# Output projection of prompt tiles 0 to 4 moved into the mixer steps of a two-layer hybrid decoder kernel

## What is computed

```python
def trunk_layer(x, ...):
    xn = rmsnorm(x, norm_mix)
    (...) = split_cols(xn @ w_in)                  # 1024 -> 2644 columns
    y_a, ... = rglru_mixer(...)                    # 256 wide, recurrent
    y_b = attn_fn(q, k, v, qi, ki, wi)             # 512 wide, top-256 sparse attention
    y_c, ... = gla_mixer(...)                      # 256 wide, linear attention
    x = x + jnp.concatenate([y_a, y_b, y_c], axis=-1) @ w_out   # 1024 x 1024
    hid = rmsnorm(x, norm_mlp) @ w_up              # 1024 -> 4096
    x = x + jnp.square(jax.nn.relu(hid)) @ w_down
    return x, ...
```

## Time and profile before

| | us |
|---|---|
| runs | 4073.2, 4067.2, 4069.69 (median 4069.69) |
| the profiled execution, first to last instruction | 4072.7 (no other time of it is shown) |
| mixer steps 3 to 7 of layer 0, by the starts of their L1109 | 92.3, 94.5, 101.5, 107.0, 116.3 long |
| output stage of layer 0, first L1382 to first L1389 | 134.0 |

### The profile page before, as it was taken

How to read it: one execution, slowest core, us unless ns; L and a number is a source line. 1 busy time by engine, 2 the same in 40 slices (tenths; PEclk the granted TensorE clock), 3 DMA queues, 4 the chain that set the end, 5 groups by cost and what they waited for, 6 DMA issues and landing times.

```text
span 4072.7 us, 52249 instructions
## 1 busy us (share of the span) xinstructions
PE 3569.3 (88%) x17850; PEld 2698.7 (66%) x17850; DVE 2124.8 (52%) x4881; ACT 1018.2 (25%) x2269; POOL 474.9 (12%) x637
## 2 busy tenths in 40 slices
PE   5778778888799999999987787787787999999999
PEld 3545555556447999999855554555464489999997
DVE  1347778877523444434323577887773334343344
ACT  2232333233401111111123233333234011111110
POOL 0100000221301000000001000002122000000000
PEclk9888888775999999999998888876768999999999
DMA  4000000237621111111410000002465201111111
GB/s 137 15 21 14 14 11 9 46 56 140 208 80 52 42 42 42 54 51 42 140 46 22 14 14 14 11 14 60 41 173 183 88 32 57 48 42 42 42 42 55
DMA packets 189759, 229.61 MB, mean 56 GB/s; under 512 B 72723, under 2 KB 150613, under 8 KB 189493
## 3 DMA queue, kind: packets, MB, share of 16 engines
q1 hardware_dynamic: 161796, 165.17, 15.1%
q0 software_dynamic: 20416, 50.27, 3.9%
q10 hardware_dynamic: 7280, 10.83, 0.8%
HBM read 203.22 MB, written 22.98 MB: 56 GB/s over the span
## 4 chain that ended last, share of the span: by engine, by line
PE 74%; DVE 10%; issue 5%; ACT 5%; DVEq 2%; SPq 1%; DMA 1%; POOLq 1%; POOL 1%; ACTq 0%
PE bank L1389 13%; PE bank L1390 13%; PE bank L1391 13%; PE bank L1096 10%; PE bank L1382 6%; PE bank L1092 5%; PE bank L1194 4%; DVE arena L1454 2%; ACT arena L709 2%; PE bank L1178 2%; DVE arena L1721 1%; PE bank L1186 1%; PE bank L1307 1%; PE bank L1140 1%; SPq L464 1%
## 5 line engine op out<-in xcount | busy, mean ns | idle before, releaser
L1861 DVE TENSOR_TENSOR x_rows<-x_rows,bank 128x512 f32<-128x512 f32 (+1 forms) x576 | 396.1, 688 | 632.1 <-PE bank L1391 632.1
L1096 PE MATMUL bank<-arena 128*128 128x512 f32 (+5 forms) x1440 | 526.5, 521 | 3.0 <-ACT arena L737 1.5
L1454 DVE TENSOR_SCALAR_CACHE_REDUCE arena<-arena,vectors 128x384 bf16<-128x384 f32 (+7 forms) x434 | 500.0, 1152 | 47.5 <-POOLq L406 15.3
L709 ACT ACTIVATE arena<-bank 128x512 f32<-128x512 f32 (+11 forms) x848 | 325.1, 440 | 772.3 <-PE bank L1096 334.0
L1389 PE MATMUL bank<-xT_hi,w_up_hi 128*128 128x364 f32 (+1 forms) x1536 | 506.0, 329 | 5.3 <-DVE vectors L1842 5.3
L1391 PE MATMUL bank<-xT_hi,w_up_lo 128*128 128x364 f32 (+1 forms) x1536 | 506.0, 329 | 0.0
L1390 PE MATMUL bank<-xT_lo,w_up_hi 128*128 128x364 f32 (+1 forms) x1536 | 505.9, 329 | 0.0
L1389 PE MATMUL bank<-w_down_hi,hidden_hi 128*128 128x512 f32 x1152 | 449.5, 390 | 7.5 <-issue 7.5
L1390 PE MATMUL bank<-w_down_lo,hidden_hi 128*128 128x512 f32 x1152 | 449.6, 390 | 0.0
L1391 PE MATMUL bank<-w_down_hi,hidden_lo 128*128 128x512 f32 x1152 | 449.6, 390 | 0.0
L1096 PEld LDWEIGHTS bank<-arena 128*128 128x128 f32 (+1 forms) x1440 | 254.5, 194 | 254.8 <-issue 226.4
(11 more groups left out here) (251 smaller groups left out, 4369.4 us busy)
## 6 DMA issues: line engine op xcount, KB each, us to landing
w_up_landing<-in_w_up SPq DMA_DIRECT2D x32, 1024.0 KB, 7.3
w_down_landing<-in_w_down SPq DMA_DIRECT2D x32, 1024.0 KB, 4.9
arena<-in_cache_k SPq DMA_DIRECT2D x160, 128.0 KB, 2.7
arena<-in_cache_v SPq DMA_DIRECT2D x160, 128.0 KB, 2.6
arena<-in_cache_v POOLq DMA_DIRECT2D x96, 128.0 KB, 3.1
arena<-in_cache_k POOLq DMA_DIRECT2D x96, 128.0 KB, 2.9
arena<-in_w_in ACTq DMA_DIRECT2D x4, 2048.0 KB, 16.1
out_projection<-in_w_out SPq DMA_DIRECT2D x16, 512.0 KB, 9.7
```

Of the source, the lines that this page charges most:

```text
L709: return act.activation(dst, src, ACT.Copy, scale=scale)
L1096: ins = mm(b[:R, o:o + w], xnT[:, c, 0:R], w_in[:, c, c0:c0 + w], start=c == 0, stop=c == 7)
L1454: ts(junk, sc, cf[:R].bitcast(F32), None, ALU.is_ge, ALU.add, accum_out=cnt[:R])
L1861: tt(x, x, b[P - R:P, :], ALU.add).then_inc(s_took, 1)
```

## The change

`EARLY = 5`: for tiles a = 0 to 4 the product y @ w_out leaves the output stage and is done in mixer step s = a + 3, as four bursts of 256 columns (8 products each): op0 and op1 in slot 0, op2 in slot 2, op3 in slot 8. A quarter of w_out (1 MB) is loaded by SyncE into the one buffer wq before each burst. ScalarE copies the burst's bank into one of two buffers `part`, and a GpSimd DMA adds it to x in `x_scratch` in DRAM (in layer 0 the prompt's first 640 rows are copied there first). The attention transposes `yb` move from slot 1 to slot 0, the attention parts of tiles 0 to 4 are no longer stored, and the output order changes. The SBUF for it (3072 columns) comes from a smaller scratch area for GpSimd's DMAs.

```diff
-OUT_ORDER = (0, NT) + tuple(range(1, NT))
+EARLY = 5
+OUT_ORDER = (0, NT, 2, 5, 1, 3, 6, 4, 7)
...
+def projects(s):
+    return s - 3 if 0 <= s - 3 < EARLY else None
...
+                if h == 0:
+                    if attends(s - 1) is not None:
+                        act.append((l, attends(s - 1), "yb"))
+                    if projects(s) is not None:
+                        act += [(l, projects(s), "op0"), (l, projects(s), "op1")]
...
+                    sp.dma_start(x_scr[0:EARLY * P, :], D["x_prompt"].rearrange("a t d -> (a t) d")[0:EARLY * P, :]).then_inc(s_xcp, 16)
...
+                def load_quarter(a, q):
+                    if q:
+                        sp.wait_ge(s_full_a, A_AT[l, a, f"op{q - 1}"] + 1)
+                    elif a or l:
+                        sp.wait_ge(s_full_a, A_AT[(l, a - 1, "op3") if a else (l - 1, EARLY - 1, "op3")] + 1)
+                    sp.dma_start(wq, D["w_out"][l].rearrange("(c p) n -> p c n", p=P)[:, :, 256 * q:256 * q + 256]).then_inc(s_wq, 16)
+                    if q == 0:
+                        sp.wait_ge(s_yst, T(l, a) + 1)
+                        for i, c in enumerate((0, 6)):
+                            sp.dma_start(yac[:, 2 * i:2 * i + 2, :], y_scr[a].rearrange("p (c r) -> p c r", c=8)[:, c:c + 2, :]).then_inc(s_yac, 16)
+                load_x(1)
+                for s in range(TILES - 1):
+                    a = projects(s)
+                    if a is not None:
+                        for q in (1, 2):
+                            load_quarter(a, q)
+                    if s + 2 < TILES:
+                        load_x(s + 2)
+                    if a is not None:
+                        load_quarter(a, 3)
+                    if projects(s + 1) is not None:
+                        load_quarter(projects(s + 1), 0)
...
+                    if t == 7:
+                        sp.wait_ge(s_full_d, D_AT[l, 5, "r1"] + 1)
                         sp.dma_start(yTl[:, t % 2, :, :], y_scr[t].rearrange("p (c r) -> p c r", c=8)).then_inc(s_y[t % 2], 16)
                     if t == 1:
                         sp.wait_ge(s_full_d, D_AT[l, NT, "r1"] + 1)
-                    sp.dma_start(xall[:R, t, :], x_src(l, t)).then_inc(s_xr[t], 16)
+                    if t == 0:
+                        for i in range(2):
+                            sp.wait_ge(s_acc[i], 16 * part_n(l + 1, 0, 0) // 2)
+                    sp.dma_start(xall[:R, t, :], x_scr[t * P:(t + 1) * P, :] if t < EARLY else x_src(l, t)).then_inc(s_xr[t], 16)
                     if t == 0:
                         sp.dma_start(gml, D["norm_mlp"][l].partition_broadcast(P)).then_inc(s_gml, 16)
-                    if t == 1:
+                    if t == 5:
                         load_up(0)
...
+                def add_part(a, q):
+                    pool.wait_ge(s_evac, A_AT[l, a, f"op{q}"] + 1)
+                    pool.dma_start(x_scr[a * P:(a + 1) * P, 256 * q:256 * q + 256], part[:, q % 2, :], accum_op=ALU.add).then_inc(s_acc[q % 2], 16)
                 rstd(0)
+                if l == 0:
+                    pool.wait_ge(s_xcp, 16)
...
+                            add_part(projects(s), q)
                     if s == NT:
                         pool.wait_ge(s_pt, 16 * (l + 1))
@@ -627,11 +695,13 @@
                         load_ki(3)
                     if s + 1 < TILES:
                         rstd(s + 1)
-                    if attends(s - 1) is not None:
+                    if attends(s - 1) is not None and attends(s - 1) >= EARLY:
                         a = attends(s - 1)
                         pool.wait_ge(s_evac, A_AT[l, a, "yb"] + 1)
                         store(y_part(a, 2, 4), yB)
                         stored(s_ybst)
+                    if projects(s) is not None:
+                        add_part(projects(s), 2)
...
+                                add_part(projects(s), 3)
                             pool.wait_ge(s_evac, A_AT[l, t, "yc"] + 1)
                             store(y_part(t, 6, 2), yC[:, t % 2, :, :])
...
+                def part_out(a, q):
+                    n = part_n(l, a, q)
+                    if n >= 2:
+                        act.wait_ge(s_acc[q % 2], 16 * (n // 2))
+                    b = take((l, a, f"op{q}"))
+                    copy(part[:, q % 2, :], b[:, 0:256]).then_inc(s_evac, 1)
...
+                        if h == 0 and attends(s - 1) is not None:
+                            a = attends(s - 1)
+                            if l * (NT - EARLY) + max(a - EARLY, 0):
+                                act.wait_ge(s_ybst, l * (NT - EARLY) + max(a - EARLY, 0))
+                            b = take((l, a, "yb"))
+                            copy(yB, b[:, :].rearrange("p (c r) -> p c r", c=4)).then_inc(s_evac, 1)
...
+                        if h == 0 and projects(s) is not None:
+                            for q in range(2):
+                                part_out(projects(s), q)
...
+                                part_out(projects(s), 2)
                             if P_:
                                 decay_logits(s)
...
                                 project(s + 1, 7)
+                            if projects(s) is not None:
+                                part_out(projects(s), 3)
                             if P_:
                                 R = rows(s)
                                 b = take((l, s, "yc"))
...
+                    if t < EARLY:
+                        act.wait_ge(s_xr[t], 16 * (l + 1))
+                    else:
+                        act.wait_ge(s_took, D_AT[l, t, "r1"] + 1)
...
+                def project_out(a, q):
+                    pe.wait_ge(s_wq, 16 * (part_n(l, a, q) + 1))
+                    if q == 0:
+                        pe.wait_ge(s_yac, 32 * (l * EARLY + a + 1))
+                        evac((l, a, "yb"))
+                    b = a_bank((l, a, f"op{q}"))
+                    for c in range(8):
+                        y = yB[:, c - 2, :] if 2 <= c < 6 else yac[:, c if c < 2 else c - 4, :]
+                        ins = mm(b[:, 0:256], y, wq[:, c, :], start=c == 0, stop=c == 7)
+                    ins.then_inc(s_full_a, 1)
...
+                        if h == 0 and attends(s - 1) is not None:
+                            attention_T(attends(s - 1))
                         if h == 1:
-                            if attends(s - 1) is not None:
-                                attention_T(attends(s - 1))
                             if P_:
                                 heads_T(s)
                         if h == 2:
+                            if projects(s) is not None:
+                                project_out(projects(s), 2)
                             if P_:
...
                             probs_T(A_, h - 1)
                         if h < 7 and A_ is not None:
                             logits(A_, h + 1)
+                        if h == 0 and projects(s) is not None:
+                            for q in range(2):
+                                project_out(projects(s), q)
                         if h >= 1 and A_ is not None:
                             values(A_, h - 1)
...
                             if N_:
                                 project(s + 1, 7)
+                            if projects(s) is not None:
+                                project_out(projects(s), 3)
                             if P_:
                                 R = rows(s)
                                 pe.wait_ge(s_yc, T(l, s) + 1)
...
+                    for n in range(2 if t >= EARLY else 0):
                         b = d_bank((l, t, f"r{n}"))
...
-                                pe.wait_ge(s_xT, 2 * (TILES * l + min(TILES, (c0 + w + P - 1) // P + 1)))
+                                pe.wait_ge(s_xT, 2 * (TILES * l + order_covers(range(c0 // P, (c0 + w + P - 1) // P))))
...
-    nc = _bacc.Bacc("TRN2", target_bir_lowering=False, num_devices=1)
+    nc = _bacc.Bacc("TRN2", target_bir_lowering=False, num_devices=1, dynamic_dma_scratch_size=4096)
...
```

More of the change, by code:

```diff
@@ L57, in selects, with order_covers @@
     return s - 1 if 2 <= s - 1 < NT else None
+def projects(s):
+    return s - 3 if 0 <= s - 3 < EARLY else None
+def order_covers(tiles):
+    return max(OUT_ORDER.index(t) for t in tiles) + 1
 def rows(t):
@@ L94, in plan @@
                 if h == 2:
+                    if projects(s) is not None:
+                        act.append((l, projects(s), "op2"))
                     if P_:
@@ L131, in plan @@
                         act.append((l, s + 1, "G3"))
+                    if projects(s) is not None:
+                        act.append((l, projects(s), "op3"))
                     if P_:
@@ L212, in program @@
         ARENA = (53215 - const_cols - 288 - 16) // 8 * 8
+        AHEAD0 = ARENA
+        ARENA += 2048 + 512 + 512
         arena_at = (nc.sbuf_base + 31) // 32 * 32
@@ L519, in _ @@
                 sp.wait_ge(s_full_a, A_AT[l, "s", "PT2.4"] + 1)
```

(14 more changed lines are left out.)

27 lines of the change are left out of this document (12 added, 15 removed).

## The result

The changed kernel took 4124.5 us (median of 4 runs, 4111.4 to 4132.6) beside 4068.4 us for the kernel before on the same chip: ratio 1.0143, 95% interval 1.0116 to 1.0169. The forecast was 4044. The profiled execution has a span of 4130.9 us against 4072.7, 58.2 longer.

What follows compares the result with a forecast made beforehand. TensorE was taken to bound the kernel (74% of the work that ended last). Terms: -96 + 70 + 10 - 10 = -26 us, 4046.7 against the profiled 4072.7, 4044 beside the median; range 3995 to 4095.

Steps and rivals of the forecast that it cites:

- Output stage, -96: Output stage: five of nine products go, less four holes of 4.2 us and three slow starts; -48.0 us a layer.
- Chain of slot 0, 25.15 us: Steps 4 to 7, G3 to L1109: op3 3.55, load 5.7, op0 5.25, load 5.4, op1 5.25 us.
- `norm_x` late by 2.4 us less than L1109: GpSimd's root 2.1 us after op1, so 6.7 late; 8.0 a step for eight steps, 3.0 for two: +70 us.
- Bursts at 5.25 us after a wait: Bursts in slot 0: 3.55 us at 2.4 GHz plus 1.7 for a slow start; bounds of the addition 0 and 3.55.
- op2 +10, clock -10: Slots 1 to 3: op2 ahead of slot 2's transposes +1 us a step; work after dense bursts -1 a step.
- Edits costed at nothing: Moved transposes, GpSimd's additions and waits, heads' root, x loads, copy of x, smaller scratch: 0 us.
- the second one: Single buffer: waits of op0 and op1 for wq ahead of L1109 make it slower, 4091 to 4138 us; chance 0.22.
- its point of decision: The single-buffer rival decides from 9.6 us a step on, since the output stage returns 96 over ten steps; forecast had 7.
- Its recorded sign: For the single-buffer rival: steps longer by over 10 us with a granted clock near 0.5 in the bursts.
- The first rival: TensorE's holes really take the bursts: loads at 4.9 us, bursts at 2.4 GHz throughout; 3994 to 4010 us; chance 0.15.

Runs made afterwards that it cites:

- the two experiments on it: Changed kernel with GpSimd's root ahead of both additions: 4075.2 us; or with the root behind product 1's copy but ahead of its addition: 4081.7 us.
- no_reload: Changed kernel with only the first quarter of w_out loaded in each layer, so other bursts use wrong weights: 3991.7 us, ratio 0.9814.
- spread: Changed kernel with the root ahead of the additions, product 3 ahead of G3, product 1 in slot 1, product 2 in slot 2: 3977.4 us, ratio 0.9791.
- late_wait: Changed kernel with the root first, product 3 ahead of G3, and GpSimd's wait for y stores behind the next heads' root: 4016.4 us, ratio 0.9880.

## Why the prediction was wrong, point by point

*Output stage, -96.* Right: -94.9, holes and slow starts included. (The terms that it names, 4.9 less 1.0, make holes of 3.9 us, nearer the measured than its 4.2.)

*Chain of slot 0, 25.15 us.* Right in its kind, short in size: 26.5 to 27.7, on average 27.2, from G3 to the heads' transposes in steps 4 to 7. Two terms were too small: the first quarter's load, 6.8 us on average against 5.7, because the second of its y loads lands last, and the two bursts (next paragraph but one). The row of the table is off by 9.5 us in layer 0, 6.3 of it in steps 4 to 7, 1.4 in step 3 and 1.7 in step 8, which was forecast as unchanged; in layer 1 it is off by 13.8. The median of the quarter loads is 5.4 us on the page, as taken from the earlier trace rows. The Trainium skill's fit for the GpSimd path ("DMA: Bandwidth & Descriptors", the anatomy of one DMA) gave 4.4 as an estimate; the trace does not agree with it on SyncE's queue.

*`norm_x` late by 2.4 us less than L1109.* **This is the step that failed.** The text had it "2.1 after op1", made of the copy, the issue and the root, each from a row. The instructions were all there and in that order; what was missing is the `drain` inside the root, which came just behind a freshly issued DMA. Measured 7.0. It turned -12 us a layer into +14, that is 52 of the 89 us by which the steps were off, and the two experiments on it returned 49 and 43.

*Bursts at 5.25 us after a wait.* Right in kind, short in size: the 18 that waited for a load in slot 0 took 5.2 to 6.8 us, 5.9 on average, 12 us more in all than forecast; step 6 above has the shortest product 0 (5.69) and the shortest product 1 (5.19). The mean over all 40 is 5.0. The means of 0.65 and 0.70 above hide two levels; product 0 of step 6 in two pieces:

```profile
608.27:611.00 2.73, 2.73 (x7) 2.19 (x8) 0.00 (x0) 0.00 (x0) 1.88 (x2) 0.50 0.00 0
612.50:613.96 1.46, 1.46 (x7) 0.95 (x5) 1.31 (x4) 0.00 (x0) 0.00 (x0) 1.00 0.00 0
```

The burst begins at 1.2 GHz, behind the wait, and ends at 2.4.

*op2 +10, clock -10.* Their sum was forecast as 0 and came out at 5.7 us in layer 0 and 2.0 in layer 1, inside the bounds; G3 adds 4.8 in layer 0, since three of six took 8.55 to 9.53 us where before only the last did (8.49), and 1.1 in layer 1, where two of six were slow before as well. That a slower clock would reach G3 was not in the text. What lowers it there was only seen, not tested.

*Edits costed at nothing.* For the heads' root it held: VectorE waited longer for it, but TensorE's L1199 did not wait. That no more than GpSimd's issue of an addition would be on a path did not: its aftermath in the queue was.

*The rivals.* The outcome lies in the second one, slower and with 4091 to 4138, and its point of decision was right: 9.6 us a step, and 15.9 came. Its place, the waits for wq ahead of L1109, is shown by no_reload. Its price was not: it wanted the 18 bursts at 1.2 GHz to their end, 7.1 us each, and they took 5.9; and it wanted product 2 in the path at 7.1 us, where all from `norm_x` to the next G3 rose by 5.7 and 2.0 us a layer. Its recorded sign came in part: four of the five steps 3 to 7 of layer 0 were 14.7 to 18.8 us longer, but the granted clock in the bursts shown was 0.65 and 0.70 and not near 0.5. The first rival, that the holes take the bursts, needed what spread has: one burst to a slot and no wait for a load in slot 0; then 3977 us were measured, below that rival's 3994. The forecast put 0.65 on faster because it took the chain's lateness as the only give-back and let VectorE come out of it early.

## What to carry to other kernels

Where a moved instruction lands on a queue, read what stands directly behind it: here GpSimd, which issued a DMA and then had a `drain`, paid for that DMA there, so dependent small work goes ahead of the issue. With a single buffer the order (use, other work, use) decides: four bursts of 3.7 us and their 1 MB loads cost 159 us in the places and the order of the change (43 to 49 of it through the root), and about 2 us spread over slots 8, 0, 1 and 2 with the root first. A second buffer was not tried. Before giving up a change that lost, ask which of its parts paid as forecast (here the output stage, to 1 us) and place the rest anew.

## What was unexpected of the hardware

- A `drain` on GpSimd behind an addition to DRAM issued 0.9 us before took 4.1 to 4.6 us (4.49 at 631.15), 2.1 to 2.3 us in no_reload, where the addition before that one was issued 2 to 3 us earlier and not 11, and 0.24 us where the addition came after it. Behind a fresh plain store (late_wait, 580.74) it was 1.45 us. What sets the length was not tried.
- The wait for the last y store ahead of the heads' root grew in step 6 from 2.73 to 5.52 us with an addition issued just ahead of that store, and was 1.65 us in step 6 of spread, where product 3's addition comes earlier. What it costs in the changed kernel was not tried.
- A product of 16 matmuls of 256 columns took 3.7 us after a wait of 0.36 us and 5.2 to 6.8 us when TensorE had just waited for 4.5 to 5.7 us. In spread the same holds some 6 us after a wait: product 1 at 571.78 took 5.38 us. Windows around products 0 and 1 there (columns as in the earlier trace rows):

```profile
555.60:559.40 3.80, 3.69 (x16) 2.96 (x16) 2.96 (x9) 1.66 (x4) 1.75 (x3) 1.00 0.09 37
571.70:577.20 5.50, 5.50 (x20) 4.56 (x19) 4.61 (x16) 0.00 (x0) 0.00 (x0) 0.68 0.00 0
```

The granted clock is 1.00 in the first and 0.68 in the second window, behind the 6.59 us wait at 565.95. It is a mean over the window, of the levels 1.2 and 2.4 GHz.
